# Searching all key sides in the query stage of a two-block token kernel, with three gathered rows per slot

## The reference

```python
q = (xi @ w_q).reshape(n, PEER_HEADS, 2, PEER_KEY_DIM)        # 8 heads, 2 sides, 128
s = jnp.einsum('nhpc,hpkc->nhpk', q, sub_keys)                # 128 scores a side
ts, ti = lax.top_k(s, PEER_TOPK)                              # best 16 a side
cand_s = ts[:, :, 0, :, None] + ts[:, :, 1, None, :]          # 256 pairs a head
best_s, best_p = lax.top_k(cand_s, PEER_TOPK)                 # best 16 pairs a head
idx = jnp.take_along_axis(cand_i, best_p, axis=-1)
gate = jax.nn.softmax(best_s, axis=-1)
act = jax.nn.gelu(jnp.einsum('nd,nhkd->nhk', xi, u[idx]), approximate=False)
out = jnp.einsum('nhk,nhkd->nd', gate * act, v[idx])
```

## Time and profile before

| | us |
|---|---|
| median of 3 runs | 2338.49 |
| lowest, highest run | 2335.31, 2339.03 |
| span of the profiled execution | 2339.2 |
| query stage, first to last scores | 424 to 513 |
| route stage, u tiles 0 to 91 on PE | 517.7 to 917.4 |
| gate matrices | 917.4 to 1125 |
| expert groups | 1193 to about 1690 |

### The profile page before, as it was taken

The page is one execution under the profiler, slowest core; times in us unless marked ns, Lnnn a source line. Parts: engine busy times, 40 slices in busy tenths (PEclk is TensorE's granted clock), DMA queues, the critical chain, the costliest instruction groups (busy, mean ns, idle before and its releaser), DMA issues.

```text
span 2339.2 us, 31291 instructions
## 1 busy us (share of the span) xinstructions
PE 2182.7 (93%) x12743; PEld 1269.1 (54%) x12743; DVE 1528.4 (65%) x2558; ACT 897.1 (38%) x1066; POOL 729.7 (31%) x540
## 2 busy tenths in 40 slices
PE   6999889998999988999999999999879998999998
PEld 5464554444665555777656555555545455444444
DVE  4557763248979999999578888888767174433002
ACT  5333552333343324566433333333232354444110
POOL 2311001312414242222133343343417401544540
PEclk9999989998999999999999999999979999999999
DMA  5223552225877776877899999999722211233310
GB/s 200 73 73 141 183 181 72 91 73 193 320 251 289 276 284 227 324 285 286 321 356 376 377 380 381 378 379 380 250 101 73 101 49 37 73 108 108 144 36 36
DMA packets 194479, 483.39 MB, mean 207 GB/s; under 512 B 10672, under 2 KB 93648, under 8 KB 188320
## 3 DMA queue, kind: packets, MB, share of 16 engines
q1 hardware_dynamic: 154624, 334.65, 40.3%
q0 software_dynamic: 39712, 146.74, 16.6%
HBM read 428.92 MB, written 52.43 MB: 206 GB/s over the span
## 4 chain that ended last, share of the span: by engine, by line
PE 53%; DVE 24%; DMA 15%; ACT 3%; issue 3%; POOL 1%; SPq 1%; DVEq 0%; ACTq 0%; POOLq 0%
PE psum L559 14%; PE psum L560 14%; PE psum L561 14%; DMA expert_act<-act_dram 12%; DVE weight_low L1988 6%; DVE row_sum L2217 2%; PE psum L961 2%; DMA rows_b<-peer_v_dram,row_index 2%; POOL weight_low L2538 1%; DVE hidden_low L2384 1%; PE psum L753 1%; DVE expert_act L2379 1%; DVE rows_a L2204 1%; DVE rows_b L2204 1%; PE psum L844 1%
## 5 line engine op out<-in xcount | busy, mean ns | idle before, releaser
L559 PE MATMUL psum<-x_high,weight_high 128*128 128x384 bf16 (+3 forms) x1856 | 650.5, 350 | 37.6 <-DVE weight_low L1988 23.3
L560 PE MATMUL psum<-x_low,weight_high 128*128 128x384 bf16 (+3 forms) x1856 | 649.1, 350 | 0.0
L561 PE MATMUL psum<-x_high,weight_low 128*128 128x384 bf16 (+3 forms) x1856 | 648.5, 349 | 0.0
L1275 ACT ACTIVATE weight_high<-weight_stage 128x4096 bf16<-128x4096 f32 (+2 forms) x100 | 356.2, 3562 | 237.6 <-PE psum L561 119.2
L2538 POOL TENSOR_TENSOR weight_low<-weight_stage,weight_high 128x512 bf16<-128x512 f32 (+1 forms) x229 | 300.0, 1345 | 428.1 <-ACT weight_high L1275 428.0
L559 PE MATMUL psum<-hidden_high,weight_high 128*128 128x384 bf16 x1024 | 334.9, 327 | 10.7 <-DVE hidden_low L2384 10.7
L560 PE MATMUL psum<-hidden_low,weight_high 128*128 128x384 bf16 x1024 | 334.9, 327 | 0.0
L561 PE MATMUL psum<-hidden_high,weight_low 128*128 128x384 bf16 x1024 | 334.8, 327 | 0.0
L1988 DVE TENSOR_TENSOR weight_low<-weight_stage,weight_high 128x4096 bf16<-128x4096 f32 x69 | 304.8, 4418 | 35.8 <-ACT weight_high L1275 35.8
L559 PEld LDWEIGHTS psum<-x_high,weight_high 128*128 128x128 bf16 (+1 forms) x1856 | 185.9, 100 | 201.6 <-DVE weight_low L1988 27.6
L561 PEld LDWEIGHTS psum<-x_high,weight_low 128*128 128x128 bf16 (+1 forms) x1856 | 185.5, 100 | 158.0 <-issue 12.1
(11 more groups left out here) (350 smaller groups left out, 2983.1 us busy)
## 6 DMA issues: line engine op xcount, KB each, us to landing
weight_stage<-peer_u_dram SPq DMA_DIRECT2D x32, 2048.0 KB, 8.6
weight_stage<-peer_v_dram SPq DMA_DIRECT2D x32, 2048.0 KB, 11.7
weight_stage<-mlp_w_dram SPq DMA_DIRECT2D x16, 2048.0 KB, 8.0
weight_stage<-ada_w_dram SPq DMA_DIRECT2D x12, 2048.0 KB, 8.0
act_dram<-norm_value SPq DMA_DIRECT2D x128, 192.0 KB, 9.9
gate_dram<-gate_matrices SPq DMA_DIRECT2D x12, 2048.0 KB, 12.0
gates<-gate_dram SPq DMA_DIRECT2D x32, 768.0 KB, 16.9
expert_act<-act_dram SPq DMA_DIRECT2D x32, 768.0 KB, 18.6
```

Source lines behind the costliest of these rows:

```text
L559: self.nc.tensor.matmul(out, left[0], right[0], start=first, stop=False)
L560: self.nc.tensor.matmul(out, left[0], right[1], start=False, stop=False)
L561: return self.nc.tensor.matmul(out, left[1], right[0], start=False, stop=last)
L1275: nc.scalar.activation(k.block_view(m.w_high, n % SPLITS, n), k.block_view(m.w_stage, n % STAGES, n), ACT.Copy).then_inc(*s.w_high.up(n))
```

## The change

All four token tiles are searched as each side's scores arrive in the query stage (`SIDES_EARLY` = 16), so that `best_side` and its indices hold four tiles. The route stage keeps ten slots a tile: 8 pair searches and the 2 one-hot steps. Three rows are consumed in each slot of o > 0, 30 a tile instead of 24, and all later row numbers move up by 18. The low half of u0 still stands behind side 14, those of u1 and u2 behind the first pair search and behind the one-hot steps of o = 0. The low halves of o > 0 are spread over ten slots instead of 24. `pair_places` now shares memory with `pair_scores`.

```diff
-        self.best, self.best_i = m("best_side", [P, 2 * PH, TOPK]), m("best_side_index", [P, 2 * PH, TOPK], U32)
+        self.best, self.best_i = (m(name, [P, QT, 2 * PH, TOPK], dtype) for name, dtype in (
+            ("best_side", F32), ("best_side_index", U32)))
...
-LOWS_ROUTE = [[(14 <= _x) + (16 <= _x) for _x in range(3 * PH)] + [3]]
-for _end in ROUTE_ENDS:
+SIDES_EARLY = 16
+LOWS_QUERY = [int(14 <= _x) for _x in range(2 * PH)]
+ROUTE_SLOTS = [PH + 2] + [2 * PH - SIDES_EARLY + PH + 2] * (QT - 1)
+LOWS_ROUTE = [[2] * ROUTE_SLOTS[0] + [3]]
+for _end, _slots in zip(ROUTE_ENDS, ROUTE_SLOTS[1:]):
     _low, _high = LOWS_ROUTE[-1][-1], (_end - 6) // EG + 2
-    LOWS_ROUTE.append([_low + (_high - _low) * (_x + 1) // (3 * PH) for _x in range(3 * PH)] + [_end // EG + 1])
+    LOWS_ROUTE.append([_low + (_high - _low) * (_x + 1) // _slots for _x in range(_slots)] + [_end // EG + 1])
...
-ROWS_ROUTE = [3 * PH * _o for _o in range(QT)]
+ROWS_SLOT = 3
+ROWS_ROUTE = [ROWS_SLOT * ROUTE_SLOTS[1] * _o for _o in range(QT)]
...
+    def sides(self, o, hp):
+        m, t = self.m, ROUTE_TILES[o]
+        self.top16(m.score[:, t, hp, :], m.best[:, o, hp, :], m.best_i[:, o, hp, :])
+
+    def slot(self, o):
+        if o > 0:
+            self.rows(ROWS_ROUTE[o - 1] + ROWS_SLOT * (self.slots + 1))
+        self.low_parts(LOWS_ROUTE[o][self.slots])
+        self.slots += 1
...
+        for hp in range(2 * PH):
+            nc.vector.wait_ge(*s.act_out.at("keys", hp))
+            for o in range(QT if hp < SIDES_EARLY else 1):
+                self.sides(o, hp)
+            self.low_parts(LOWS_QUERY[hp])
         for o, t in enumerate(ROUTE_TILES):
...
-            for hp in range(2 * PH):
-                if o == 0:
-                    nc.vector.wait_ge(*s.act_out.at("keys", hp))
-                self.top16(m.score[:, t, hp, :], m.best[:, hp, :], m.best_i[:, hp, :])
-                if o > 0:
-                    self.rows(ROWS_ROUTE[o - 1] + hp + 1)
-                self.low_parts(LOWS_ROUTE[o][hp])
...
             for h in range(PH):
                 self.top16(m.cand[:, h, :], m.pair[:, h, :], m.pair_i[:, 0, h, :])
-                if o > 0:
-                    self.rows(ROWS_ROUTE[o - 1] + 2 * PH + h + 1)
-                self.low_parts(LOWS_ROUTE[o][2 * PH + h])
+                self.slot(o)
...
+                self.slot(o)
-            self.low_parts(LOWS_ROUTE[o][3 * PH])
+            self.low_parts(LOWS_ROUTE[o][-1])
```

More of the change, by code:

```diff
@@ L252, in __init__ @@
         self.query = m("queries", [P, 2, SEQ])
-        self.best, self.best_i = m("best_side", [P, 2 * PH, TOPK]), m("best_side_index", [P, 2 * PH, TOPK], U32)
-        self.best_f, self.cand = m("best_side_index_bf", [P, 2 * PH, TOPK], BF16), m("pair_scores", [P, PH, N_PAIRS])
+        self.best, self.best_i = (m(name, [P, QT, 2 * PH, TOPK], dtype) for name, dtype in (
+            ("best_side", F32), ("best_side_index", U32)))
+        self.best_f = m("best_side_index_bf", [P, 2 * PH, TOPK], BF16)
+        before_pairs = m.at
+        self.cand = m("pair_scores", [P, PH, N_PAIRS])
         self.pair, self.shifted = m("best_pair", [P, PH, TOPK]), m("best_pair_shifted", [P, PH, TOPK])
-        self.pair_i, self.place = m("best_pair_index", [P, 3, PH, TOPK], U32), m("pair_places", [P, 4, PH, TOPK])
+        self.pair_i = m("best_pair_index", [P, 3, PH, TOPK], U32)
+        self.place = Map(nc, before_pairs)("pair_places", [P, 4, PH, TOPK])
         self.rank, self.pick = m("best_rank", [P, 2, PH, TOPK], BF16), m("picks", [P, 3, PICKS])
@@ L270, in __init__ @@
         after_scores = m.at
+        assert after_scores - 2 * 4 * D >= hot.at
         rows_a = Map(nc, free)("rows_a", [P, 2, D])
@@ L2271, in route @@
             [P, TOPK, TOPK])).then_inc(*step.up())
+        for hp in range(2 * PH):
[3 more added lines that the diff above has]
+            self.low_parts(LOWS_QUERY[hp])
         for o, t in enumerate(ROUTE_TILES):
[L2273 to L2276, removed]
+            self.slots = 0
             if o > 0:
-                nc.vector.wait_ge(*step.now())
-            for hp in range(2 * PH):
-                if o == 0:
-                    nc.vector.wait_ge(*s.act_out.at("keys", hp))
-                self.top16(m.score[:, t, hp, :], m.best[:, hp, :], m.best_i[:, hp, :])
-                if o > 0:
-                    self.rows(ROWS_ROUTE[o - 1] + hp + 1)
-                self.low_parts(LOWS_ROUTE[o][hp])
+                for hp in range(SIDES_EARLY, 2 * PH):
+                    self.sides(o, hp)
+                    self.slot(o)
+                nc.vector.wait_ge(*(s.routed.at("row_lists") if o == 1 else s.copied.at("picks", ROUTE_TILES[o - 1])))
             nc.vector.wait_ge(*step.now())
-            nc.vector.tensor_copy(m.best_f[:, :, :], m.best_i[:, :, :]).then_inc(*step.up())
-            sides = m.best[:, :, :].rearrange("p (h s) k -> p h s k", s=2)
+            nc.vector.tensor_copy(m.best_f[:, :, :], m.best_i[:, o, :, :]).then_inc(*step.up())
+            sides = m.best[:, o, :, :].rearrange("p (h s) k -> p h s k", s=2)
             for lo, end, n, at in PAIRS:
```

## The result

The changed kernel takes 2381.05 us (median of four, 2374.15 to 2381.59), the one before 2336.9 on the same chip: 1.0176 times as long, 95% interval 1.0157 to 1.0194. The prediction was 2369, with a range of 2350 to 2382, and 0.88 for slower.

A forecast was written before the change was run, and what follows sets the result against it. Route stage bound by when DVE finishes each block's low half; 20.2 + 7.0 + 7.7 - 2 - 1.5 = +31 us, 2370.6 on the profiled 2339.2, about 2369 beside the median; range 2350 to 2382 (8 in 10).

The forecast's parts named there:

- Searches moved: Query stage: a side takes DVE 6.88 us, scores come every 6.07; PE starts u0 15.6 us later, row lists 20.7 later.
- First stop: Route stage up to PE's stop for o = 1: u3's low half late, stop at 711 against 691.0, +20 us.
- o = 2 and 3: Route stage stretches: 122 and 119 us against 115.0 and 111.4, +7 and +7.7 us.
- Gate stage and experts: Gate stage gives back 2 us of clock; last four expert groups, without rows, give -1.5 us.
- likeliest outcome: Whole kernel: slower by +24 to +38 us, range 2362 to 2376, chance 0.60.
- The step that failed: Route stage: row requested right before a low half is held 4.88 us, lands at 14.5; period 19.2 us instead of 14.0.
- A: DVE keeps up with PE in o = 2 and 3, deciding at 1.6 us row wait a period; 2332 us, chance 0.12.
- B: Only the start costs, +20 us, o = 2, 3 as before; 2357; chance 0.16 with what lies toward no change.
- C: Gathers slow one another in the route stage: period 21.5 us, +43 us in all, 2382; chance 0.12.

## Why the prediction was right, and where it was not

**Searches moved: right.** u0's low half was forecast to begin at 528.9; it began at 524.38, in an execution whose query stage was 3.8 us early, so 0.7 us ahead of the forecast. The row lists were done at 572.9 (577.3 less 3.8 is 573.5). A search takes 1.70 us there.

**First stop: right in kind, 2.7 us short.** From PE's wait in the query stage to the stop it is 290.7 us, 267.8 before: +22.9, forecast +20.2. Up to u3 all was in time (594.8, forecast 600 less 3.8). I had then let PE run freely for 28 tiles; it waited 2.3 us at u5 and 1.2 at u8, and the clock in that stretch is 0.95. And what costs is not the start but the lists, with u3 behind them: with u0 early nothing was gained, and with 12 sides early the first stop came 20.6 us sooner than with 16 (24 rows a tile in both).

**o = 2 and 3: right.** 122.5 and 119.6, forecast 122 and 119; low halves of o = 3 18.6 to 19.1 apart, forecast 19.2; the picks not waited for; u22 26.2 us behind the block before, forecast 26.1. Beside the kernel before one thing stands out that the sum does not say: there the low halves of o = 3 were 18.7 to 18.8 apart too. From the stop to u21 the changed kernel takes 75.2 us, the one before 76.4; from u21 to the next stop 44.5 and 35.0. So the period kept the change from gaining in o = 3, and the 8.3 us lost there lie at u22, whose half now stands behind `places`, both one-hot steps and six rows. PE in the kernel before, and after (two lines):

```profile
882.42 0.34 PE L559 MATMUL psum<-x_high,weight_high 128*128 128x384 bf16 x1 [1.36 <-DVE weight_low L1988]
```

```profile
907.62 0.34 PE L564 MATMUL psum<-x_high,weight_high 128*128 128x384 bf16 x1 [1.86 <-DVE weight_low L1997]
933.77 0.50 PE L564 MATMUL psum<-x_high,weight_high 128*128 128x384 bf16 x1 [10.38 <-DVE weight_low L1997]
```

**Gate stage and experts.** 205.0 for 206.0 (forecast -2), and +0.6 for the groups (forecast -1.5). That last term was wrong in sign: four groups without rows gave nothing.

The parts measured sum to 22.9 + 7.3 + 8.3 - 1.0 + 0.6 - 0.6 (what follows the groups) = +37.5; forecast was +31. The medians are 44 apart, outside the likeliest outcome's own range (+24 to +38) and 1 us inside the upper end of the whole one; that it is inside is partly luck. Where the last 6.7 us lie is not shown: the other three executions of the changed kernel are 6.6 to 7.4 us longer than the profiled one, and only their spans are known. A later query stage, as in the run with u0 early, would account for 5.5 of it.

**The step that failed** is the reason given for the period: "PE's stops" and "19.2" came from "If that happens right before a low half, POOL's issue takes 4.88 us", the row asked for then landing at 14.5. The landings were right (13.8, 15.7 and 17.5 us after the half began at 865.35, forecast 14.5, 16.2 and 18.0), but the hold does not make the period. Half the instruction took the hold away (row there after 6.1 us) and left the period at 18.7. What the runs show in its place: between two low halves DVE uses six rows, the ring can hold four, and a row asked for while the 2 MB move lands 8.5 us after its request. Which of the six meets the wait changes with the order of issue; that there is one does not. The number of rows decides: with six it is 18.7 us, with four 15.6, at PE's pace; with none, PE's pace too. The load is a part (1.4 us for half of it). The DMA engines are busy 84 to 91% of a period with six rows, which moves 6.0 MB (rows, load and PE's tiles stored). Their bytes alone are not it, as the half load shows; how much comes of the trips one behind another, and how much of the ring's depth, which no run varied, stays open. The prediction did not read the DMA share at all, though the earlier trace rows has it.

**Rivals.** A's condition was never met (row waits of 4.3 us in the period shown, where it allowed 1.6). B is out: o = 2 and 3 took 7.3 and 8.3 us more than before, and two rows a slot gave 39.6 us back. C's price was near the measured total for the wrong reason: one of the three requests behind a half was indeed held by a row's instruction (1.74 us at 872.56), but the rows landed no later than forecast and the period was 18.7, not 21.5.

## What to carry to other kernels

Moving work into an idle stretch pays as long as the consumer behind it is still in time: 12 of 16 sides were free, all 16 cost 17 us of route more (24 rows a tile in both). What is put in the place of the removed work needs its own sum: here the number of gathered rows between two fixed points decided more than DVE's time did. The low half that stands last in its stage should be counted with everything that now stands ahead of it, as u22's was late for `places`, the one-hot steps and six rows. And a part moved to a later stage must be priced there too: half a row more in each expert group cost 30 us, where PE was busy 98% and the DMA share 1.01; that these two are the cause was only inferred.

## What the runs showed of the hardware

An indirect DMA's issue on POOL takes 0.94 us, 1.74 when it begins during a row's instruction on DVE (1.2 us), 4.88 beside a 4.42 us `tensor_tensor`, and 2.75 when that is cut into two of 2.2: each time it ended 0.8 to 0.9 us behind the DVE instruction that was running when it began (865.70 + 4.88 = 870.58, the half ended at 869.77). An issue that began first was not held: 0.94 us at 900.00, with a row's instruction from 900.19 on. The Trainium skill (SBUF — State Buffer, "Who interferes with whom") infers that descriptor generation is not held up by `tensor_tensor`; these runs say it is, here.

In 1.4 us slices of three periods the changed kernel's DMA engines moved up to 436 GB/s (the kernel before has one slice of 453 between 855 and 910), and 364 over the expert groups of the kernel before, where the view gives a share of 1.01. The Trainium skill (Perfetto Trace Analysis, "Roofline") gives about 435 GB/s as the bound of a core's 16 DMA engines; the highest slices lie at that figure within 4%, and the long stretch stays well below.

```profile
GB/s 151 186 407 436 424 335 417 418 402 413 425 259 17 116 186 395 424 415 295 410 398 382 414 419 386 35 0 186 337 413 433 352 388 409 408 418 416 362 169 0
```

A wait of PE costs more than itself: with three and five waits for low halves PE's granted clock is 0.97 and 0.91 in o = 2 and 3 of the change, 1.00 in both without rows.
